# Spreading the routing weights over 64 expert tiles in a two-block transformer kernel

## The reference

```
q = h @ w_q                          # 8 heads, 2 halves of 128
s = q . subkeys                      # 128 scores per half
v, i = top_k(s, 16)                  # per half
cand = v0 + v1 ; tv, tj = top_k(cand, 16)     # 16 experts of 16384 per head
w = softmax(tv)
a = gelu(h . w_down[expert])
out = sum over head and k of (w * a) * w_up[expert]
x = x + ga2 * out                    # ga2: one row of 1024 gates
return rms_norm(x)
```

## Time and profile before

| | us |
|---|---|
| median of the runs | 2104.67 |
| the profiled execution (its span) | 2105.0 |
| lead tiles, from 1201 to 1300 | about 99 |
| routing stage and row of gates, 1300 to 1447.6 | 147.6 |
| pairs, 1447.6 to 1993.1 | 545.5 |
| last tiles, 1993.1 to 2092.0 | 98.9 |
| after the last matmul | 13.0 |

### The profile page before, as it was taken

The page is one execution under the profiler, slowest core; times in us unless marked ns, Lnnn a source line. Parts: engine busy times, 40 slices in busy tenths (PEclk is TensorE's granted clock), DMA queues, the critical chain, the costliest instruction groups (busy, mean ns, idle before and its releaser), DMA issues. The chain is left out here.

```text
span 2105.0 us, 31928 instructions
## 1 busy us (share of the span) xinstructions
PE 1876.6 (89%) x10718; PEld 1607.2 (76%) x10718; DVE 1321.8 (63%) x2412; ACT 889.9 (42%) x1329; POOL 319.6 (15%) x210
## 2 busy tenths in 40 slices
PE   7767999889997999699697997768999999999997
PEld 6646998677567997577456996667999999999875
DVE  4546566665556654755555998996656656656655
ACT  4543443444223443444424444664444444444432
POOL 0202000200212000212021798330000000000000
PEclk9888999898578999889758999888999999999999
DMA  7503557476233555334203453001555555555553
GB/s 264 187 25 125 182 184 262 171 256 234 90 111 125 179 183 188 119 122 152 80 0 126 145 180 130 0 0 62 188 185 183 189 182 186 189 181 188 180 170 119
DMA packets 85537, 317.03 MB, mean 151 GB/s; under 512 B 9520, under 2 KB 9776, under 8 KB 84832
## 3 DMA queue, kind: packets, MB, share of 16 engines
q1 hardware_dynamic: 76464, 278.43, 38.6%
q10 hardware_dynamic: 7776, 26.50, 3.5%
q0 software_dynamic: 1232, 11.24, 1.4%
HBM read 315.08 MB, written 1.05 MB: 150 GB/s over the span
## 5 line engine op out<-in xcount | busy, mean ns | idle before, releaser
L200 DVE TENSOR_TENSOR wl<-ring,wh 128x1024 fp32r<-128x1024 f32 x481 | 591.9, 1232 | 541.1 <-ACT wh L198 540.5
L198 ACT ACTIVATE wh<-ring 128x1024 fp32r<-128x1024 f32 x529 | 560.2, 1060 | 860.9 <-PE bank L222 797.6
L220 PE MATMUL bank<-xh,wh 128*128 128x256 f32 x1880 | 539.9, 287 | 19.8 <-DVE xl L324 9.2
L221 PE MATMUL bank<-xl,wh 128*128 128x256 f32 x1880 | 535.8, 285 | 0.0
L222 PE MATMUL bank<-xh,wl 128*128 128x256 f32 x1880 | 535.2, 285 | 0.0
L220 PEld LDWEIGHTS bank<-xh,wh 128*128 128x128 f32 x1880 | 364.0, 194 | 30.5 <-issue 8.1
L221 PEld LDWEIGHTS bank<-xl,wh 128*128 128x128 f32 x1880 | 364.7, 194 | 4.3
L222 PEld LDWEIGHTS bank<-xh,wl 128*128 128x128 f32 x1880 | 364.2, 194 | 0.0
L220 PE MATMUL bank<-wh,wa_high 128*128 128x512 f32 x512 | 204.5, 399 | 5.8 <-DVE wa_low L1683 5.8
L221 PE MATMUL bank<-wl,wa_high 128*128 128x512 f32 x512 | 202.2, 395 | 0.0
L222 PE MATMUL bank<-wh,wa_low 128*128 128x512 f32 x512 | 201.5, 394 | 0.0
(11 more groups left out here) (416 smaller groups left out, 2317.5 us busy)
## 6 DMA issues: line engine op xcount, KB each, us to landing
ring<-in_stream SPq DMA_DIRECT2D x529, 512.0 KB, 3.3
ada<-in_w_ada ACTq DMA_DIRECT2D x48, 512.0 KB, 3.5
rows<-in_rows POOLq DMA_DIRECT2D x2, 2560.0 KB, 11.3
con<-in_early POOLq DMA_DIRECT2D x1, 2078.0 KB, 10.7
x_feature_major<-in_x_fm ACTq DMA_DIRECT2D x4, 256.0 KB, 7.9
x<-in_x_tm POOLq DMA_DIRECT2D x1, 1024.0 KB, 8.6
weighted<-in_subkeys POOLq DMA_DIRECT2D x1, 1024.0 KB, 5.2
out<-weighted SPq DMA_DIRECT2D x2, 512.0 KB, 2.7
```

The costliest lines, as they stand in the source:

```text
L198: C.activation(wh[q % AHEAD][:, :], ring[slot][:, :], ACT.Copy).then_inc(s_high, 1)
L200: low.tensor_tensor(wl[q % AHEAD][:, :], ring[slot][:, :], wh[q % AHEAD][:, :], ALU.subtract).then_inc(s_low, 1)
L220: T.matmul(o, left[0], right[0], start=start, stop=False, skip_group_check=True)
L221: T.matmul(o, left[0], right[1], start=False, stop=False, skip_group_check=True)
```

## The change

The lead tiles are now 36 (`FIRST`). The next 64 tiles each stand beside one routing group: the program issues, in 64 unrolled steps, the group's PE product and one expert down product, then the one-hot rows of the next group, the ACT copy of the previous group, the split of a piece three ahead (low part on POOL), the gelu of this tile, and the DVE multiplies. `LEAD` is then 100 (36 + 64), so 28 pairs and 100 last tiles remain. In a routing step g some tokens already have their weight when tile 36+g gets its gelu, and others do not. The gelu is made in two pieces, and DVE multiplies the early tokens (`late_weigh`). The two turns of the chosen indices stand before tile 34. The row of gates is made inside the last tiles, ahead of the last ten.

```diff
-LEAD = 32
+FIRST = 36
+TB = 4
+ROUTES = S // TB
+LEAD = FIRST + ROUTES
-turn_route(0, IJ[:, 0], picked, iT)
-turn_route(1, IJ[:, 1], picked, jT)
-for u in range(LEAD - LEAD % BODY, LEAD):
+for u in range(FIRST - BODY, FIRST):
+    if u == FIRST - 2:
+        turn_route(0, IJ[:, 0], picked, iT)
+        turn_route(1, IJ[:, 1], picked, jT)
     lead_tile(u, None)
 rdone = turn_route(2, Wt, wd, wT)
...
+def onehots(g):
+    o_i, o_j = oh_i[g % 2], oh_j[g % 3]
+    if g >= 2:
+        V.wait_ge(s_wp, g - 1)
+    for k in range(TB):
+        last = V.tensor_scalar(o_i[:, k, :], iota, iT[:, one], wT[:, one], ALU.is_equal, ALU.mult)
+    if g % 4 == 3:
+        V.wait_ge(s_wp, g - 2)
+        V.tensor_tensor(o_j[:, :, :], iota_b, j_b, ALU.is_equal).then_inc(s_oj, 1)
+    else:
+        if g >= 3:
+            G.wait_ge(s_wp, g - 2)
+        G.tensor_tensor(o_j[:, :, :], iota_b, j_b, ALU.subtract).then_inc(s_dj, 1)
+        C.wait_ge(s_dj, by_pool + 1)
+        C.activation(o_j[:, :, :], o_j[:, :, :], ACT.Abs).then_inc(s_aj, 1)
+        C.wait_ge(s_aj, 2 * by_pool + 1)
+        C.activation(o_j[:, :, :], o_j[:, :, :], ACT.Relu, scale=-1.0, bias=1.0).then_inc(s_aj, 1)
+def route_copy(g):
+    lo = FIRST + g + 1
+    C.wait_ge(s_wp, g + 1)
+    C.activation(WA[:, lo:NE, TB * g:TB * g + TB], by_tile(g)[:, lo:NE, :], ACT.Copy).then_inc(s_wc, 1)
+def route_multiply(g):
+    hi = FIRST + g + 1
+    V.tensor_tensor(dst, dst, by_tile(g)[:, 0:hi, :], ALU.mult).then_inc(s_wm, 1)
+def late_gelu(g):
+    v, n = FIRST + g, TB * g
+    C.wait_ge(s_used, q1 + g + 1)
+    if n:
+        C.activation(act_g[v % 3][:, 0:n], bank[4 + v % 3][:, 0:n], ACT.Gelu_apprx_tanh)
+    C.activation(WA[:, v, n:S], bank[4 + v % 3][:, n:S], ACT.Gelu_apprx_tanh).then_inc(s_gelu, 1)
+def late_weigh(g):
+    V.tensor_tensor(WA[:, v, 0:n], WA[:, v, 0:n], act_g[v % 3][:, 0:n], ALU.mult).then_inc(s_late, 1)
+onehots(0)
+for g in range(ROUTES):
+    route_product(g)
+    down(q1 + g, 0, FIRST + g, 0)
+    if g + 1 < ROUTES:
+        onehots(g + 1)
+    if g >= 1:
+        route_copy(g - 1)
+    split(q1 + g + AHEAD, low=G)
+    late_gelu(g)
+    if g >= 2:
+        route_multiply(g - 2)
+    if g >= 3:
+        late_weigh(g - 2)
...
-ga2, ga2_done = row_of(ga2, sb(diag_scope, "ga2_diag", [P, KD, P]), 5 * KD)
...
 with nc.Fori(1, LEAD // BODY - 1, ...) as i:      # the last tiles
     ...
+ga2, ga2_done = row_of(WA[:, 16:20, :]..., WA[:, 12:16, :]..., 5 * KD)
 for v in range((LEAD // BODY - 1) * BODY, LEAD):
     last_tile(v, None)
```

More of the change, by code:

```diff
@@ L1380, in build @@
     wT = sb(peer, "route_w", [P, S])
-    spare = WA[:, LEAD:NE, :].rearrange("p j t -> p (j t)")
+    spare = WA[:, FIRST:NE, :].rearrange("p j t -> p (j t)")
     taken_to = [0]
@@ L1468, in build @@
         lead_tile(u, None)
-    with nc.Fori(1, LEAD // BODY, engines=(ENG.PE, ENG.Activation, ENG.Pool)) as i:
+    with nc.Fori(1, FIRST // BODY - 1, engines=(ENG.PE, ENG.Activation, ENG.Pool)) as i:
         for u in range(BODY):
             lead_tile(u, i)
-    q1 = q0 + LEAD
     cand = carve(PH, TOPK * TOPK)
@@ L1556, in build @@
     scope = ExitStack()
[L1557 to L1560, removed]
+    act_g = [sb(scope, f"gelu{i}", [P, S]) for i in range(3)]
+    route_scope = ExitStack()
+    oh_i = [sb(route_scope, f"onehot_i{i}", [P, TB, NE]) for i in range(2)]
+    oh_j = [sb(route_scope, f"onehot_j{i}", [P, TB, NE]) for i in range(3)]
     s_oi = nc.alloc_semaphore("onehot_i_done")
@@ L1567, in build, with made_ahead @@
     s_wm = nc.alloc_semaphore("route_multiplied")
+    s_late = nc.alloc_semaphore("late_tile_weighed")
     dve.wait(rdone)
-    V.wait_ge(s_gelu, LEAD)
+    act.wait(rdone)
     pool.wait(rdone)
[L1572 to L1582, removed]
+    q1 = q0 + FIRST
+    def made_ahead(g):
+        return g // 4, 3 * (g // 4) + g % 4
+    def onehots(g):
+        toks = slice(TB * g, TB * g + TB)
+        o_i, o_j = oh_i[g % 2], oh_j[g % 3]
+        if g >= 2:
+            V.wait_ge(s_wp, g - 1)
         for k in range(TB):
-            one = slice(tok + k, tok + k + 1) if i is None else bass.ds(tok + k, 1)
+            one = slice(TB * g + k, TB * g + k + 1)
             last = V.tensor_scalar(o_i[:, k, :], iota, iT[:, one], wT[:, one], ALU.is_equal, ALU.mult)
@@ L1588, in route_group @@
         j_b = jT[:, toks].unsqueeze(2).broadcast_to([P, TB, NE])
-        if u == GROUPS - 1:
+        by_dve, by_pool = made_ahead(g)
+        if g % 4 == 3:
+            V.wait_ge(s_wp, g - 2)
             V.tensor_tensor(o_j[:, :, :], iota_b, j_b, ALU.is_equal).then_inc(s_oj, 1)
         else:
-            v = r * (GROUPS - 1)
+            if g >= 3:
+                G.wait_ge(s_wp, g - 2)
             G.tensor_tensor(o_j[:, :, :], iota_b, j_b, ALU.subtract).then_inc(s_dj, 1)
-            C.wait_ge(s_dj, v + (u + 1))
+            C.wait_ge(s_dj, by_pool + 1)
@@ L1596, in route_group, with route_product @@
             C.activation(o_j[:, :, :], o_j[:, :, :], ACT.Abs).then_inc(s_aj, 1)
-            C.wait_ge(s_aj, v * 2 + (2 * u + 1))
+            C.wait_ge(s_aj, 2 * by_pool + 1)
             C.activation(o_j[:, :, :], o_j[:, :, :], ACT.Relu, scale=-1.0, bias=1.0).then_inc(s_aj, 1)
-        T.wait_ge(s_oi, n + (u + 1))
-        if u == GROUPS - 1:
-            T.wait_ge(s_oj, r + 1)
-        else:
-            T.wait_ge(s_aj, v * 2 + (2 * u + 2))
-        if i is not None:
-            T.wait_ge(s_wm, n + (u - GROUPS + 1))
+    def route_product(g):
+        by_dve, by_pool = made_ahead(g)
+        T.wait_ge(s_oi, g + 1)
+        if g % 4 == 3:
+            T.wait_ge(s_oj, by_dve + 1)
+        else:
+            T.wait_ge(s_aj, 2 * by_pool + 2)
+        if g >= 4:
+            T.wait_ge(s_wm, g - 3)
@@ L1606, in route_group @@
         for k in range(TB):
-            last = T.matmul(b[:, k * P:(k + 1) * P], o_i[:, k, :], o_j[:, k, :], start=True, stop=True,
-                            skip_group_check=True)
+            last = T.matmul(bank[g % 4][:, k * P:(k + 1) * P], oh_i[g % 2][:, k, :], oh_j[g % 3][:, k, :],
+                            start=True, stop=True, skip_group_check=True)
         last.then_inc(s_wp, 1)
[L1611 to L1652, removed]
@@ L1653, in build, with by_tile @@
-    diag_scope = ExitStack()
-    ga2, ga2_done = row_of(ga2, sb(diag_scope, "ga2_diag", [P, KD, P]), 5 * KD)
[L1655 to L1658, removed]
+    def by_tile(g):
+        return bank[g % 4][:, :].rearrange("p (t j) -> p j t", t=TB)
+    def route_copy(g):
+        lo = FIRST + g + 1
+        C.wait_ge(s_wp, g + 1)
+        C.activation(WA[:, lo:NE, TB * g:TB * g + TB], by_tile(g)[:, lo:NE, :], ACT.Copy).then_inc(s_wc, 1)
@@ new lines, in route_multiply @@
+    def route_multiply(g):
+        hi = FIRST + g + 1
+        dst = WA[:, 0:hi, TB * g:TB * g + TB]
+        V.wait_ge(s_wc, g + 1)
+        V.wait_ge(s_gelu, hi)
+        V.tensor_tensor(dst, dst, by_tile(g)[:, 0:hi, :], ALU.mult).then_inc(s_wm, 1)
[3 more added lines that the diff above has]
+        if n:
+            if g >= 4:
+                C.wait_ge(s_late, g - 3)
+            C.activation(act_g[v % 3][:, 0:n], bank[4 + v % 3][:, 0:n], ACT.Gelu_apprx_tanh)
+        C.activation(WA[:, v, n:S], bank[4 + v % 3][:, n:S], ACT.Gelu_apprx_tanh).then_inc(s_gelu, 1)
@@ new lines, in late_weigh @@
+    def late_weigh(g):
+        v, n = FIRST + g, TB * g
+        V.wait_ge(s_gelu, v + 1)
+        V.wait_ge(s_wc, g)
+        V.tensor_tensor(WA[:, v, 0:n], WA[:, v, 0:n], act_g[v % 3][:, 0:n], ALU.mult).then_inc(s_late, 1)
[13 more added lines that the diff above has]
+            late_weigh(g - 2)
@@ L1659, in build @@
+    route_copy(ROUTES - 1)
+    for g in (ROUTES - 2, ROUTES - 1):
+        route_multiply(g)
+        late_weigh(g)
+    for lane in (act, dve, pool):
+        lane.wait((s_wc, ROUTES), (s_wm, ROUTES), (s_late, ROUTES - 1))
+    route_scope.close()
+    q1 = q1 + ROUTES
     wah = [sb(scope, f"wa_high{i}", [P, S], F32R) for i in range(3)]
@@ L1709, in pair @@
         parts(u + 1, n, None if i is None and u < 2 else q - 2, s)
+        if i is None and u == 0:
+            T.wait_ge(s_wm, ROUTES)
         up(q + 1, s, u, n)
@@ L1720, in build @@
             pair(u, i)
-    assert (NE - LEAD) % PB == 0
+    for u in range((NE - LEAD) // PB * PB, NE - LEAD):
+        pair(u, None)
     q2 = q1 + 2 * (NE - LEAD)
@@ L1741, in build @@
             last_tile(v, i)
+    ga2, ga2_done = row_of(WA[:, 16:20, :].rearrange("p j t -> p (j t)"),
+                           WA[:, 12:16, :].rearrange("p j (a n) -> p (j a) n", a=2), 5 * KD)
     for v in range((LEAD // BODY - 1) * BODY, LEAD):
```

## The result

The changed kernel takes 2169.38 us (median of 4 runs, 2160.04 to 2179.2). The kernel before, beside it, took 2103.79. The ratio is 1.031, with a 95% interval of 1.026 to 1.036: the change makes the kernel slower by 3.1%. The forecast was 2164. It is estimated from all single times and so is not the quotient of two medians (for e4 that would be 0.995 and not 0.990), and differences of half a per cent are not to be relied on.

What follows compares the result with a forecast made beforehand. A ring through ACT's and POOL's in-order queues was taken to bound the routing block. From 1300.1: + 11.5 + 6.9 + 359 (routing) + 159.0 (pairs) + 309 (last tiles) + 5.5 + 13.0 = 2164 us; 80% range 2132 to 2196.

Steps and rivals of the forecast that it cites:

- The ring: Routing block: split, low part, subtract, Abs, Relu, copy, next split through ACT's and POOL's in-order queues; 6.01 us a turn.
- closed steps: Routing steps whose split waits on POOL's subtract through Abs, Relu and copy: 46 of 62 intervals, 6.01 us each.
- The rival that PE sets the step: Routing block: ACT and POOL run ahead, step is PE's 3.88 us, total 2056, faster; chance 9%.
- PE's step: Routing block: PE's work per step, product 1.0 plus down tile 2.88, 3.88 us.
- open steps: Routing steps where DVE makes the j row and the split waits only for PE: 16 intervals, 3.88 us each.
- the 9 us that I had added for delays between DVE and POOL: Routing block: waiting DVE instructions slip between POOL's low part and subtract; 0.15 x 62 = 9 us.
- +14: Routing block at clock 0.82: PE step 4.7, +0.85 us in each of 16 open steps; the upper bound, not summed.
- a fall for the whole block: Rival, routing block: lower clock makes PE's step 7.0 us, block 448, total 2253; chance 5%.
- DVE's one-hots would not come into the ring: Routing block: DVE's four TENSOR_SCALAR fit POOL's 2.6 us idle; rival adds about 1 us per closed step, 2210, chance 7%.
- Moving tiles out of pairs: Last tiles: 68 tiles moved out of pairs cost 68 x (3.09 - 2.77) = 22 us.
- The row of gates: Last tiles: PE's row product waits for eight DVE products; 5.5 us, where before it was 7.0.
- The hand-over to the pairs: From routing block to pairs: 0.8 us to the last tiles; PE's pieces in hand cover the wait, if not 2 us.

Runs made afterwards that it cites:

- e4: Changed kernel with each piece's low part made by DVE, not POOL, in the routing block; POOL keeps its subtracts; 2082.77 us, 0.990 of the kernel before.
- e1: Changed kernel with POOL making each onehot_j subtract twice in the routing block; 2225.46 us, 1.057 of the kernel before.
- e2: Changed kernel with POOL's subtract issued one step earlier, ahead of a low part, same instructions; 2083.88 us, 0.995 of the kernel before.
- e3: Changed kernel with onehot_j made by DVE in all 64 groups, without POOL's subtracts and ACT's Abs and Relu; 2070.54 us, 0.988 of the kernel before.
- e9: e3 with the row 0..127 copied once into PSUM and read there by DVE's one-hots; 2042.55 us, 0.974 of the kernel before.
- e10: e9 plus weight parts two tiles ahead in the last tiles and PE's row of gates two tiles behind DVE's products; 2009.95 us, 0.957 of the kernel before.
- e6: Changed kernel with 12 extra unread PE matmuls before each routing product whose j row comes from POOL; 2159.92 us, 1.029 of the kernel before.
- e5: Changed kernel with DVE making the weights' high and low parts two tiles ahead, not one, in the last tiles; 2134.61 us, 1.018 of the kernel before.
- e7: Kernel before with only the row of gates moved into the last tiles, ahead of the last eight; 2092.86 us, 0.998 of the kernel before.

## Why the prediction was right

- **The time.** The median is 5 us above the forecast of 2164, but the profiled execution, to which the terms belong, is 14 above (2177.9): 8 of them in the routing block, the rest in terms that I had a little too low. That the median came so near is in part luck: the other executions were shorter by 7 to 19 us.
- **The ring.** Right, link by link: 6.01 forecast, 5.9 to 6.2 measured in the 46 closed steps. e1 lengthened one link and paid for it in every round; e2, e3 and e4 open the ring in three ways and each took back 85 to 95 us. The rival that PE sets the step is dead for the changed kernel. It is true in e9 and e10, where the ring and the wait of the one-hots behind POOL are both gone.
- **PE's step.** 3.76, and not 3.88: eight product records and 24 matmuls follow one another at 0.12 us, so a product costs PE 0.88 and not the 1.0 that I took.
- **The clock.** Right in the closed steps, where its falls are hidden (6.0 at either level). The term for the open steps was mis-sized: I took 3.88 and bounded it at 4.7 from the mean clock of the old stage; ten of them took 5.5. The mean was no worse than I had bounded it (0.92 to 0.93), but the low time fell in the open steps, where PE is the bound. The rows show why: in the open step from 1451.15 to 1456.70 the product alone took 1.73 at the lower level of 1.2 GHz, after three closed steps with 2.0 to 2.3 us of idle each, and in the steps around it 1.05 to 1.13 at 2.4 GHz. The open steps together came to 79.9 us, 17.8 above 16 x 3.88; the 9 us that I had added for delays between DVE and POOL did not come (the closed steps average 6.02 with everything in them). The difference is the 8 us by which the block was longer than forecast. The rule of the Trainium skill on small idles ("TensorE: Matmul & The Clock Gate", section "A second HAM failure mode: psum-queue depth-cycling"), which I had left out of the sum at +14, was the better guide: 15.4 us came back in e6. Against a fall for the whole block I had written that a PE busy without gaps has 1.00. That does not hold everywhere: in the stretch of attention shown above PE is busy 47 of 47 us at 0.61.
- **DVE against POOL.** That DVE's one-hots would not come into the ring was right, but not for the reason given. I had put them into POOL's 2.6 us of idle time. They begin when the product ends (1457.53), just ahead of POOL's low part, and run beside it and the subtract: 4.04 us for four, ended 1.0 before Relu. So a microsecond was all that kept them out. They are the next bound as soon as the ring is cut, which I had not priced: e3 and e2 stay 31 and 41 us above e9, where the one-hots no longer wait.
- **Moving tiles out of pairs.** Forecast 22 us for 68 tiles, 0.31 each; e5 gives 29.5 for 100 tiles, 0.30 each.
- **The row of gates.** Forecast 5.5 in its new place, measured 7.0 (a split interval of 10.40 where 3.41 is usual). The row products took 3.57 us where I had halved 3.75: PE had stood idle for 3.97, and from 2130.84 to 2134.40 the granted clock was 0.55. In e10, with no such idle time, the same four took 1.88. So the whole move won nothing that e7 could tell from noise.
- **The hand-over to the pairs.** I took it as covered and named 2 us if not; PE waited 2.08.

## What to carry to other kernels

Before work is interleaved, write each engine's queue down in order for two steps and look for a path that leaves one queue, passes through another and comes back; its length is the step, however idle all engines are. Such a ring can be cut by issuing one link a step earlier; in e2 that took no further instruction and no further buffer. The second question here is which DVE instruction runs beside a long POOL instruction: where the wide input could lie in PSUM (e9), the two ran side by side. A third is where the low clock falls: it cost 1.5 us in a step that PE bounds and nothing in one that it doesn't.

## What the runs showed of the hardware

- A short DVE instruction waited for the rest of a POOL instruction: 2.15 us instead of 0.29 for a 128x132 multiply, 3.19 instead of 1.10 for four one-hots in SBUF, and 6.80 where POOL ran without a gap. It goes the other way too: POOL's low part took up to 3.06 (e2) and 3.10 (e3) where such an instruction of DVE had begun just before or with it, and 2.38 to 2.41 in e9.
- In a periodic pattern the low time of the clock can fall in the same step again and again: in the changed kernel the low time fell in the open step seven periods in a row, then in five it did not (4.04 to 4.08), then in three it did (5.64 to 5.67).
- Kernels with the same stages ahead of the experts came out of them up to 23 us apart in their profiles. In the stretch shown above this goes with the granted clock, 0.61 or 1.00: the same 16 matmuls (`kT_kw`, 64x256) have a median of 0.631 us in the changed kernel and 0.378 in e9. What tips it was not tried, and that the spread of the executions without a profile comes from there too is likely but not shown.
